# Two interleaved mixers on one core: recurrence scores and masked copies in another order, head output scaled one step later

## The chip, the cores and the metric

The kernel runs on one core of one Trainium2 chip. The metric is the device time of one execution in microseconds (us), lower is better. The engines are called PE (TensorE), DVE (VectorE), ACT (ScalarE), POOL (GpSimd) and SP (SyncE, which here only issues DMAs). Each works through its own instruction list in order and waits on semaphores.

## The reference

Two blocks (`DEPTH = 2`) of a network on 256 context tokens and 256 latent tokens, in fp32, then a gated convolution mixer and a dilated attention mixer. In each block, projections feed three token mixers: a differential attention, a gated linear recurrence (HGRN) in both directions, and a small Fourier mix.

```python
# recurrence, per direction, head and chunk of tokens
rel = where(lower, cum[t] - cum[s], -inf)
scores = einsum('td,sd,tsd->ts', q, k, exp(rel))
o = scores @ v + (q * exp(cum)) @ state
state = exp(cum_end) * state + (k * exp(cum_end - cum)).T @ v
# differential attention, per block of 128 queries and head
s = q @ k.T * DH_A ** -0.5             # two score sets, c = 0, 1
a = softmax(s[0]) - lam * softmax(s[1])
o = rms_norm(a @ v, w) * (1 - lam_init)
```

In block 0 both streams (4 tiles of 128 tokens) get an attention output, 16 pairs of a query tile and a head. In block 1 only the two latent tiles do, 8 pairs.

## The kernel before

Most of the time goes into large products with weights streamed from HBM (each fp32 weight is split into a high and a low part by ACT and DVE, and three products are summed). The change lies in two shorter stages, one per block (`li` = 0 and 1), where the recurrence and the attention run interleaved. Their weights are small; the next weights already wait in their three slots.

**Recurrence.** `hgrn` works through 8 units `i` (direction `d`, token tile `t`, 128 tokens each). In block 1 only units 4 to 7 need outputs (`is_full`), the first four only carry the state. A unit has these parts:

- `gates(i)`: PE transposes k into a PSUM bank (kT, L796), and makes four banks of gate sums (E, L801) and one of suffix sums (L805, L808). ACT takes exponentials (L1375, L1382). DVE copies kT (L1756), multiplies q or k into them (14 instructions at L1772, one at L1773) and makes the decayed keys (L1778, i < 6).
- scores: for 4 pairs `lp` of levels and both row halves `par`, PE writes one PSUM bank with 4 matmuls of 64 rows (L833), 8 banks in all. DVE copies them under masks into `ACC` (L1791, `copy_predicated`, 128x256 each, 16 per unit), one copy per half and level.
- states: PE multiplies `ACC` with the values and adds the state's part (O, L846 and L849), then makes the state's increment (SU, L856, i < 6). DVE copies O (L1808 or L1810) and updates `ST` in four 64x64 blocks (L1820 for i < 2, else L1822).

**Attention.** Step `st` of `attention` handles up to four heads at once: PE makes scores `s` of head u = st (L894), transposes the combined probabilities `aT` of u = st - 1 (L901), multiplies with v (`av`, u = st - 2, L910) and transposes the normed output `oT` of u = st - 3 (L917). DVE finds the row maximum (L1896, two; L1898 scales it by -0.125) and then scales the head output of u = st - 2 into `ON` (L1903). ACT takes the exponentials (L1416), evicts aT (L1223), squares `av` (L1434) and evicts oT (L1440). POOL makes the root of the mean square (L1139, L1141). DVE's `combine` of head u (L1875 to L1880) forms the difference of the softmaxes in place.

**Order.** `weave` merges the lists: after each `yield` of the recurrence it advances the attention so that all its steps (19 in block 0, 11 in block 1) spread over 20 yields; DVE's `combine` of the last head comes at the next yield, or at an early point (`yield True`). For one unit in block 0 this gives

```
PE   gates(i+1) | scores(i) | att a+1 | states(i) | att a+2
DVE  gates(i+1) | combine a | masked copies(i) | att a+1 | states(i) | combine a+1 | att a+2
ACT  gates(i+1) | att a+1 | att a+2
POOL root of head a-1 | root of head a
```

PSUM has 8 banks, given out in turn in PE's order (`open_group`); a bank is written again only when its last reader has counted up the semaphore `taken` of that bank. A score unit takes all 8.

## Time and profile before

| | |
|---|---|
| median of 3 runs | 2212.08 us (2209.62 to 2219.95) |
| the profiled execution's own time | 2207.61 us |
| its span in the trace | 2205.7 us |
| busy share of PE / DVE / ACT / POOL | 89% / 56% / 41% / 3% |
| mean granted TensorE clock | 0.913 of full speed |
| the two interleaved stages | about 272 to 505 us and 1169 to 1298 us |

Busy shares are means over stages with different limits. The granted clock has two levels, 1.0 (2.4 GHz) and 0.5 (1.2 GHz); a mean between them says how the stretch divides.

### The profile page before, as it was taken

Reading aid. Unit: us, or ns where it says so; the run is one execution under the profiler, and the core shown is the slowest. Engines: PE = TensorE matmul, PEld = TensorE weight load, DVE = VectorE, ACT = ScalarE, POOL = GpSimd, SP = SyncE. Lnnn points to the kernel's source line nnn. Section 1 sums busy time; section 2 is a strip of 40 time slices with the busy share of each in tenths; the row PEclk is TensorE's granted clock in tenths of the full one; section 3 lists DMA queues with packets and bytes.
Section 4 is the critical chain, followed back from the end, with each engine's and each line's share of the span. In section 5 each row is a group of like instructions: output and inputs, shape, how many; then the busy total and the mean of one; then the engine's idle time right before and its main releaser. Section 6 shows DMA issues by size and latency. Waiting matters only on the chain.

```text
span 2205.7 us, 27906 instructions
## 1 busy us (share of the span) xinstructions
PE 1956.8 (89%) x11307; PEld 1623.8 (74%) x11307; DVE 1235.3 (56%) x1928; ACT 911.8 (41%) x1213; POOL 74.3 (3%) x135
## 2 busy tenths in 40 slices
PE   4899878868899999998977887989799889999888
PEld 3678656657677777886864566987699869888777
DVE  3553365663666566355545646785566655455684
ACT  4534422222544444325344125564333435566442
POOL 0100000010100000001000010000100000000010
PEclk8899976669999999998987779999899999999998
DMA  7444200001344443323420015554466545555551
GB/s 261 168 147 153 77 1 1 1 1 58 115 153 153 153 153 115 99 81 131 135 94 1 1 57 164 190 173 153 132 186 191 172 158 160 174 165 169 142 66 39
DMA packets 211453, 261.41 MB, mean 119 GB/s; under 512 B 4657, under 2 KB 173283, under 8 KB 211071
## 3 DMA queue, kind: packets, MB, share of 16 engines
q1 hardware_dynamic: 207690, 248.34, 34.7%
q0 software_dynamic: 3232, 11.15, 2.8%
q8 instruction: 90, 1.47, 0.3%
q14 instruction: 36, 0.29, 0.0%
q10 hardware_dynamic: 405, 0.15, 0.0%
HBM read 258.50 MB, written 1.12 MB: 118 GB/s over the span
## 4 chain that ended last, share of the span: by engine, by line
PE 63%; issue 14%; DVE 12%; ACT 5%; DMA 4%; POOL 1%; SPq 0%; DVEq 0%; ACTq 0%; POOLq 0%
PE acc L627 16%; PE acc L629 15%; PE acc L628 15%; DVE scratch L1791 3%; PE acc L801 2%; PE acc L657 2%; PE acc L658 2%; ACT weights_high L1237 1%; DVE weights_low L1625 1%; PE acc L1096 1%; PE acc L846 1%; PE acc L849 1%; DVE mixer_scratch L1772 1%; PE acc L1072 1%; PE acc L1026 1%
## 5 line engine op out<-in xcount | busy, mean ns | idle before, releaser
L1625 DVE TENSOR_TENSOR weights_low<-weights,weights_high 128x2048 fp32r<-128x2048 f32 x232 | 526.6, 2273 | 590.7 <-ACT weights_high L1237 590.6
L1237 ACT ACTIVATE weights_high<-weights 128x2048 fp32r<-128x2048 f32 x232 | 439.9, 1899 | 613.8 <-DMA weights<-in_w_ada_dram 118.2
L627 PE MATMUL acc<-normed_t_high,weights_high 128*128 128x256 f32 (+1 forms) x1824 | 577.6, 317 | 5.3 <-DVE normed_t_low L1659 2.5
L628 PE MATMUL acc<-normed_t_low,weights_high 128*128 128x256 f32 (+1 forms) x1824 | 565.1, 310 | 0.0
L629 PE MATMUL acc<-normed_t_high,weights_low 128*128 128x256 f32 (+1 forms) x1824 | 563.7, 309 | 0.0
L627 PEld LDWEIGHTS acc<-normed_t_high,weights_high 128*128 128x128 f32 x1824 | 346.6, 190 | 37.1 <-DVE normed_t_low L1659 6.9
L628 PEld LDWEIGHTS acc<-normed_t_low,weights_high 128*128 128x128 f32 x1824 | 344.3, 189 | 22.6 <-issue 3.8
L629 PEld LDWEIGHTS acc<-normed_t_high,weights_low 128*128 128x128 f32 x1824 | 344.4, 189 | 20.8
L627 PE MATMUL acc<-weights_high,normed_t_high 128*128 128x512 f32 (+1 forms) x792 | 315.8, 399 | 28.0 <-DVE normed_t_low L1932 27.9
L629 PE MATMUL acc<-weights_high,normed_t_low 128*128 128x512 f32 (+1 forms) x792 | 310.1, 391 | 0.0
L628 PE MATMUL acc<-weights_low,normed_t_high 128*128 128x512 f32 (+1 forms) x792 | 309.9, 391 | 0.0
L627 PEld LDWEIGHTS acc<-weights_high,normed_t_high 128*128 128x128 f32 x792 | 152.0, 192 | 66.7 <-issue 33.2
L628 PEld LDWEIGHTS acc<-weights_low,normed_t_high 128*128 128x128 f32 x792 | 152.2, 192 | 34.7 <-issue 1.4
L629 PEld LDWEIGHTS acc<-weights_high,normed_t_low 128*128 128x128 f32 x792 | 152.0, 192 | 33.6
L1416 ACT ACTIVATE mixer_scratch<-acc,small 128x512 f32<-128x512 f32 (+1 forms) x48 | 29.1, 611 | 229.4 <-DVE small L1898 229.4
L657 PE MATMUL acc<-weights_high,conditioning_split 128*4 128x256 f32 x384 | 99.6, 295 | 16.1 <-DVE weights_low L1625 16.1
L658 PE MATMUL acc<-weights_low,conditioning_split 128*4 128x256 f32 x384 | 99.8, 295 | 0.0
L1473 ACT ACTIVATE scratch<-acc,param_columns 128x512 f32<-128x512 f32 (+1 forms) x88 | 55.6, 664 | 63.3 <-DVE arena L1979 37.9
L1791 DVE COPY_PREDICATED scratch<-level_masks_sb,acc 128x256 f32<-128x256 uint8 x192 | 74.0, 437 | 8.9 <-DVE scratch L1791 6.4
L1932 DVE TENSOR_TENSOR normed_t_low<-arena,normed_t_high 128x512 fp32r<-128x512 f32 (+1 forms) x60 | 50.3, 882 | 47.5 <-ACT normed_t_high L1452 47.4
L648 PE MATMUL acc<-wide_consts,merge_and_gates 128*128 128x128 f32 x144 | 31.5, 390 | 50.9 <-DVE merge_and_gates L1637 50.9
L1452 ACT ACTIVATE normed_t_high<-arena 128x512 fp32r<-128x512 f32 (+1 forms) x60 | 43.6, 777 | 67.1 <-PE acc L629 67.1
(218 smaller groups left out, 2064.0 us busy)
## 6 DMA issues: line engine op xcount, KB each, us to landing
weights<-in_w_ada_dram SPq DMA_DIRECT2D x48, 1024.0 KB, 5.3
weights<-in_w_up_dram SPq DMA_DIRECT2D x44, 1024.0 KB, 5.9
weights<-in_attn_w_in_dram SPq DMA_DIRECT2D x40, 1024.0 KB, 5.1
weights<-in_conv_w_in_dram SPq DMA_DIRECT2D x32, 1024.0 KB, 5.7
weights<-in_w_in_dram SPq DMA_DIRECT2D x24, 1024.0 KB, 6.4
weights<-in_w_down_dram SPq DMA_DIRECT2D x20, 1024.0 KB, 5.0
weights<-in_w_out_dram SPq DMA_DIRECT2D x8, 1024.0 KB, 5.1
weights<-in_conv_w_out_dram SPq DMA_DIRECT2D x8, 1024.0 KB, 5.1
```

Source lines behind the costliest of these rows:

```text
L627: pe.matmul(o, ah, bh, start=start, stop=False)
L628: pe.matmul(o, ah, bl, start=False, stop=False)
L629: return pe.matmul(o, al, bh, start=False, stop=stop)
L657: pe.matmul(o[0:4, 0:256], cond[:, k, :], wh[:, k, :], start=(k == 0), stop=False)
L658: last = pe.matmul(o[0:4, 0:256], cond[:, k, :], wl[:, k, :], start=False, stop=(k == KT - 1))
L801: pe.matmul(o[:, :], GL[:, t, d * 256 + p * P:d * 256 + (p + 1) * P], SM[:, d, 4 * hf:4 * hf + 4, :], start=True, stop=True).then_inc(full, 1)
L1237: act.activation(hi_slot(n)[:, 0:used], slot(n)[:, 0:used], ACT.Copy).then_inc(hi_in.sem, 1)
L1452: act.activation(HH[:, b + k:b + k + 2, lo:lo + X.shape[2]], X[:, r0 + k:r0 + k + 2, :], ACT.Copy).then_inc(part_hi.sem, 1)
L1473: act.activation(FC[:, j, a, 0:w], bank(key, w), ACT.Identity, scale=pcol(("cw", li, 1), a * FT + f), bias=pcol(("cb", li), a * FT + f)).t ...
L1625: dve.tensor_tensor(slot(n, ring_lo)[:, 0:used], slot(n)[:, 0:used], hi_slot(n)[:, 0:used], ALU.subtract).then_inc(lo_in.sem, 1)
L1791: ins = dve.copy_predicated(ACC[:, d, par, :, :], m, bank(key)[:, lv * 256:(lv + 1) * 256].rearrange("p (h n) -> p h n", h=2))
L1932: dve.tensor_tensor(HL[:, b + k:b + k + 2, c], X[:, r0 + k:r0 + k + 2, :], HH[:, b + k:b + k + 2, c], ALU.subtract).then_inc(part_lo.sem, 1)
```

## The change

Six edits, all in the two stages but the last:

1. PE's recurrence sends `scores(i)` ahead of `gates(i+1)`, and DVE's list has the masked copies of unit i first, then `combine`, then `gates(i+1)`.
2. Within a pair of levels the score matmuls go to the two row halves in turn, into two banks.
3. A masked copy covers both banks (128x512) when the two are adjacent; the pair that starts in bank 7 is still copied bank by bank. An extra wait and a semaphore count free the first bank.
4. `ST` holds 128 columns for each pair of heads, so that its update is one instruction (i < 2) or two in place of four.
5. ACT copies the head output out of PSUM into `ON` beside the squares, and DVE scales `ON` in place at the start of step st = u + 3 in place of the end of step u + 2; PE's transpose waits for that.
6. The factor 0.125 goes into the eviction of q, and the maximum is negated by the reduction, so L1898 goes. `combine` loses a wait that others imply.

```diff
-        ST = scr[:, 3584:3840].rearrange("p (d q n) -> p d q n", d=2, q=2)
+        ST = [scr[:, 3584:3840].rearrange("p (q n) -> p q n", q=2), ht_r[:, 3592:3848].rearrange("p (q n) -> p q n", q=2)]
...
+        o_squares = ht_r[:, 3336:3592].rearrange("p (b n) -> p b n", b=2)
...
-                def apply(i):
+                def scores(i):
...
-                            for par in range(2):
-                                o = open_group(("S", li, i, lp, par))
-                                r = slice(64 * par, 64 * par + 64)
-                                for lv in range(2):
-                                    level = 2 * lp + lv
-                                    for p in range(2):
-                                        c = (lv * 2 + p) * P
+                            outs = [open_group(("S", li, i, lp, par)) for par in range(2)]
+                            for lv in range(2):
+                                level = 2 * lp + lv
+                                for p in range(2):
+                                    c = (lv * 2 + p) * P
+                                    for par, o in enumerate(outs):
+                                        r = slice(64 * par, 64 * par + 64)
                                         if level == 0:
                                             zk_, zq_ = KTT[r, b, p, :], QH[r, p, cols_of(t)]
                                         else:
                                             zk_ = zq_ = XE[b][r, p, level - 1, :]
                                         last = pe.matmul(o[:, c:c + P], zk_, zq_, start=True, stop=True)
-                                last.then_inc(full, 1)
-                    yield
+                                        if lv and p:
+                                            last.then_inc(full, 1)
+
+                def states(i):
+                    d, t = un[i]
+                    b = i % 2
...
-                                    last = pe.matmul(o[:, p * 64:(p + 1) * 64], XE[b][r, p, 7, :], ST[r, d, p, :],
+                                    last = pe.matmul(o[:, p * 64:(p + 1) * 64], XE[b][r, p, 7, :], ST[d][r, p, 64 * par:64 * par + 64],
...
                 for i in range(8):
+                    scores(i)
                     if i + 1 < 8:
                         gates(i + 1)
-                    yield from apply(i)
+                    yield
+                    states(i)
...
-                        pe.wait_ge(*taken_after(("av", li, u)))
+                        pe.wait_ge(o_done.sem, o_done.after((li, u)))
...
-                            evict((name, li, 2 * h + m), X[:, 2 * h + m, l0:512], 512 - l0)
+                            key = (name, li, 2 * h + m)
+                            act.wait_ge(full, full_after(key))
+                            act.activation(X[:, 2 * h + m, l0:512], bank(key, 512 - l0), ACT.Copy,
+                                           scale=0.125 if name == "qa" else 1.0).then_inc(taken_of(key), 1)
...
-                            ins = act.activation(E2[:, u % 2, c, 0:n], bank(("s", li, u, c), n), ACT.Exp, scale=0.125,
+                            ins = act.activation(E2[:, u % 2, c, 0:n], bank(("s", li, u, c), n), ACT.Exp,
...
-                        act.activation(ON[:, u % 2, :], bank(("av", li, u), P), ACT.Square,
+                        act.activation(o_squares[:, u % 2, :], bank(("av", li, u), P), ACT.Square,
                                        scale=1.0 / math.sqrt(128.0), accum_out=ossq[:, b]).then_inc(o_sq.sem, 1)
+                        act.activation(ON[:, u % 2, :], bank(("av", li, u), P), ACT.Copy).then_inc(taken_of(("av", li, u)), 1)
...
+                def masked(i):
                     d, t = un[i]
-                    b = i % 2
-                    yield True
                     if is_full(li, i):
                         for lp in range(4):
                             dve.wait_ge(full, full_after(("S", li, i, lp, 1)))
+                            keys = [("S", li, i, lp, par) for par in range(2)]
+                            b0 = group[keys[0]] % BANKS
                             for lv in range(2):
-                                m = MASK[:, d, 2 * lp + lv, :].unsqueeze(1).to_broadcast([P, 2, P])
-                                for par in range(2):
-                                    key = ("S", li, i, lp, par)
-                                    ins = dve.copy_predicated(ACC[:, d, par, :, :], m,
-                                                              bank(key)[:, lv * 256:(lv + 1) * 256].rearrange("p (h n) -> p h n", h=2))
+                                acc = ACC[:, d, :, :, :].rearrange("p a h n -> p (a h) n")
+                                m = MASK[:, d, 2 * lp + lv, :].unsqueeze(1).to_broadcast([P, 4, P])
+                                lvs = slice(lv * 256, (lv + 1) * 256)
+                                if b0 + 1 < BANKS:
+                                    src = ps[:, b0:b0 + 2, lvs].rearrange("p a (h n) -> p a h n", h=2)
+                                    ins = dve.copy_predicated(ACC[:, d, :, :, :], m.rearrange("p (a h) n -> p a h n", a=2), src)
                                     if lv:
-                                        ins.then_inc(taken_of(key), 1)
+                                        ins.then_inc(taken_of(keys[1]), 1)
+                                        dve.wait_ge(*taken_after(keys[1]))
+                                        dve.sem_inc(taken_of(keys[0]), 1)
                                     else:
                                         ins.then_inc(vector_step, line.one())
-                                dve.wait_ge(vector_step, line.n)
+                                        dve.wait_ge(vector_step, line.n)
+                                else:
+                                    for par in range(2):
+                                        ins = dve.copy_predicated(ACC[:, d, par, :, :], m[:, 0:2, :],
+                                                                  bank(keys[par])[:, lvs].rearrange("p (h n) -> p h n", h=2))
+                                        if lv:
+                                            ins.then_inc(taken_of(keys[par]), 1)
+                                        else:
+                                            ins.then_inc(vector_step, line.one())
+                                    dve.wait_ge(vector_step, line.n)
+                                    if lv:
+                                        for key in keys:
+                                            dve.wait_ge(*taken_after(key))
                             for par in range(2):
                                 dve.wait_ge(*taken_after(("S", li, i, lp, par)))
-                    yield
+
+                def states(i):
...
-                        for p in range(2):
-                            for hh in range(2):
-                                r = slice(64 * hh, 64 * hh + 64)
-                                dst = ST[r, d, p, :]
-                                new = bank(key)[r, p * P + hh * 64:p * P + hh * 64 + 64]
-                                if i < 2:
-                                    ins = dve.tensor_copy(dst, new)
-                                else:
-                                    ins = dve.scalar_tensor_tensor(dst, dst, SE[r, b, 256 + p:257 + p], new, ALU.mult, ALU.add)
-                                if p == 1 and hh == 1:
+                        new = bank(key, 256).rearrange("p (q n) -> p q n", q=2)
+                        if i < 2:
+                            dve.tensor_copy(ST[d], new).then_inc(taken_of(key), 1)
+                        else:
+                            for p in range(2):
+                                ins = dve.scalar_tensor_tensor(ST[d][:, p, :], ST[d][:, p, :], SE[:, b, 256 + p:257 + p],
+                                                               new[:, p, :], ALU.mult, ALU.add)
+                                if p:
                                     ins.then_inc(taken_of(key), 1)
...
                 for i in range(8):
+                    masked(i)
+                    yield True
                     if i + 1 < 8:
                         gates(i + 1)
-                    yield from apply(i)
+                    yield
+                    states(i)
                     yield
                 live = range(NT) if li == 0 else range(2, NT)
...
-                    dve.wait_ge(a_max.sem, a_max.after((li, u)))
...
+                    if 0 <= st - 3 < U:
+                        u = st - 3
+                        b = u % 2
+                        dve.wait_ge(o_rs.sem, o_rs.after((li, u)))
+                        dve.wait_ge(*taken_after(("av", li, u)))
+                        dve.tensor_scalar(ON[:, b, :], ON[:, b, :], orstd[:, b:b + 1],
+                                                              1.0 - lam_init, ALU.mult, ALU.mult).then_inc(o_done.sem, 1)
...
-                            dve.tensor_reduce(arec[:, b, c:c + 1], bank(("s", li, u, c), n), AX.X, ALU.max).then_inc(vector_step, line.one())
-                        dve.wait_ge(vector_step, line.n)
-                        dve.tensor_scalar(amax[:, b, :], arec[:, b, :], -0.125, None, ALU.mult).then_inc(a_max.sem, 1)
-                    if 0 <= st - 2 < U:
-                        u = st - 2
-                        b = u % 2
-                        dve.wait_ge(o_rs.sem, o_rs.after((li, u)))
-                        dve.tensor_scalar(ON[:, b, :], bank(("av", li, u), P), orstd[:, b:b + 1],
-                                                              1.0 - lam_init, ALU.mult, ALU.mult).then_inc(taken_of(("av", li, u)), 1)
+                            ins = dve.tensor_reduce(amax[:, b, c:c + 1], bank(("s", li, u, c), n), AX.X, ALU.max, negate=True)
+                            if c:
+                                ins.then_inc(a_max.sem, 1)
+                            else:
```

## Rows read from the trace of the kernel before

**Rows 1.** Busy time by stretch; columns PE, PEld, DVE, ACT, POOL, clock, DMA.
```profile
272.31:318.58 46.27, 35.25 (x216) 25.66 (x215) 32.59 (x113) 10.89 (x25) 0.00 (x0) 0.78 0.00 1
318.58:401.28 82.70, 69.58 (x370) 51.31 (x369) 49.19 (x166) 18.92 (x62) 4.73 (x12) 0.69 0.00 1
401.28:476.08 74.80, 62.77 (x357) 45.55 (x356) 46.85 (x139) 19.25 (x56) 4.73 (x12) 0.73 0.00 1
476.08:504.79 28.71, 12.78 (x57) 10.09 (x55) 13.64 (x36) 9.39 (x28) 9.33 (x16) 0.62 0.00 1
1168.88:1201.07 32.19, 25.55 (x91) 16.90 (x92) 20.50 (x63) 8.79 (x23) 0.79 (x2) 0.66 0.00 1
1201.07:1227.63 26.56, 19.91 (x115) 14.55 (x115) 14.88 (x47) 5.00 (x13) 0.79 (x2) 0.71 0.00 1
1227.63:1298.35 70.72, 55.43 (x345) 43.11 (x344) 43.79 (x131) 17.88 (x52) 7.76 (x16) 0.78 0.00 1
```

**Rows 2.** Waits, 264 to 504 us: total us, times, longest.
```profile
DVE mixer_scratch L1903 <- POOL small L1141: 45.4, 15, 4.4
DVE scratch L1772 <- ACT scratch L1375: 13.3, 4, 4.7
```

**Rows 3.** The same view, 1165 to 1305 us.
```profile
DVE mixer_scratch L1903 <- POOL small L1141: 22.6, 7, 3.3
```

**Rows 4.** Timeline of DVE, 401 to 430 us: start, duration; idle before in brackets.
```profile
407.30 0.29 DVE L1772 TENSOR_TENSOR scratch<-scratch 128x128 f32<-128x128 f32 x1 [2.34 <-ACT scratch L1375]
...
413.70 1.58 DVE L1791 COPY_PREDICATED scratch<-level_masks_sb,acc 128x256 f32<-128x256 uint8 x4 [0.20 <-DVE scratch L1791]
...
423.74 0.35 DVE L1903 TENSOR_SCALAR mixer_scratch<-acc,small 128x128 f32<-128x128 f32 x1 [3.22 <-POOL small L1141]
...
424.77 1.22 DVE L1822 SCALAR_TENSOR_TENSOR scratch<-scratch,mixer_scratch,acc 64x64 f32<-64x64 f32 x4 [0.28 <-PE acc L856]
```

**Rows 5.** Groups by line and shape, whole run: two row maxima, and the copy.
```profile
L1896 DVE TENSOR_REDUCE small<-acc 128x1 f32<-128x512 f32 x32 | 20.6, 685 | 3.3 <-PE acc L894 1.9 <-DVE scratch L1791 1.2
L1896 DVE TENSOR_REDUCE small<-acc 128x1 f32<-128x256 f32 x16 | 6.0, 419 | 1.1 <-DVE scratch L1791 0.8 <-PE acc L894 0.2
L1791 DVE COPY_PREDICATED scratch<-level_masks_sb,acc 128x256 f32<-128x256 uint8 x192 | 74.0, 437 | 8.9 <-DVE scratch L1791 6.4 <-PE acc L917 0.4 <-PE acc L894 0.2
```

**Rows 6.** Timeline of two masked copies, DVE, 412.2 to 412.6 us.
```profile
411.93 0.76 DVE L1791 COPY_PREDICATED scratch<-level_masks_sb,acc 128x256 f32<-128x256 uint8 x2
```

**Rows 7.** Timeline of PE, 401 to 425 us.
```profile
401.85 4.69 PE L801 MATMUL acc<-wide_consts,arena 128*128 128x512 f32 x8
...
407.24 0.27 PE L833 MATMUL acc<-arena,scratch 64*128 64x128 f32 x1
407.24 0.27 PE L833 MATMUL acc<-mixer_scratch 64*128 64x128 f32 x1
...
407.57 3.93 PE L833 MATMUL acc<-mixer_scratch 64*128 64x128 f32 x52
...
418.61 0.66 PE L846 MATMUL acc<-arena,scratch 128*128 128x64 f32 x2 [1.29 <-DVE scratch L1791]
...
423.51 1.22 PE L856 MATMUL acc<-arena,mixer_scratch 128*128 128x128 f32 x4
```

**Rows 8.** Timeline of PE, 424 to 431 us.
```profile
427.71 1.09 PE L901 MATMUL acc<-wide_consts,mixer_scratch 128*128 128x128 f32 x4 [0.97 <-DVE mixer_scratch L1880]
428.59 1.91 PE L910 MATMUL acc<-arena 128*128 128x128 f32 x8
430.30 0.42 PE L917 MATMUL acc<-wide_consts,mixer_scratch 128*128 128x128 f32 x1
```

**Rows 9.** Timeline of PE, 447 to 451 us, one unit later.
```profile
447.69 0.44 PE L846 MATMUL acc<-arena,scratch 128*128 128x64 f32 x2
```

**Rows 10.** Busy time by stretch, columns as in rows 1.
```profile
404.00:414.00 10.00, 8.28 (x73) 6.19 (x72) 7.07 (x26) 2.19 (x4) 0.25 (x1) 1.00 0.00 0
414.40:431.30 16.90, 14.58 (x50) 10.87 (x50) 10.18 (x28) 4.63 (x16) 0.79 (x2) 0.50 0.00 1
```

5 lines of the change are left out of this document (4 added, 1 removed).

## Prediction

> **What bounds the kernel now.** I read the page first, then busy time by stretch: the change acts only in the two interleaved stages, 362 us in seven stretches [rows 1]. No DMA runs there (share 0.00) and the next weights already wait, so what these stages lose or gain passes to the end one for one. DVE is busy 221.5 us of the 362 (sum of the third pair of columns), PE 281.3. Neither is full: they take turns. The waits say for what. DVE waits 45.4 us in the first stage and 22.6 us in the second for POOL's root before it may scale a head output (L1903) [rows 2, 3], and 13.3 us for ACT's exponentials of the gate sums before L1772 on one of its two buffers [rows 2]. The timeline of a unit shows why [rows 4]: after the row maxima, DVE stands 3.22 us until softmax exponentials, squares and root of an older head have passed through ACT and POOL, which themselves had waited for those maxima. This happens twice a unit; before L1772 it stands 2.34 us. It hardly waits for PE (0.28 us before L1822), because PE's output products run under the root wait. So the root wait hides another, and this is what the sum must respect.
>
> **Terms of the instructions.** *Masked copies.* Two 128x256 copies take 0.76 us [rows 6] at 0.437 each [rows 5]; four and the wait behind them take 1.58 + 0.20 = 1.78 us [rows 4]. A 128x512 copy is not in the trace. Upper bound: two copies without overlap, 0.87. Lower bound: one copy plus 256 more elements, which cost a row maximum 685 - 419 = 266 ns [rows 5]: 0.70. I take 0.70, since it is the same work a column. Two of them, 0.04 between, and 0.27 behind (the 0.20 and one more count) make 1.71 us for a pair of levels: 0.07 less, 0.3 us a unit. At 0.87 a pair would take 2.05, 1.1 us a unit more than now, 13 us over 12 units. By the banks that PE's new order gives out, 6 of the 48 pairs start in bank 7 and stay as they are.
>
> The Trainium skill ("VectorE: DVE Perf Modes", section "The DRAIN you can't avoid") says that the next DVE instruction waits until the pipe is empty and that a semaphore between two costs nothing extra. Rows 6 speak against it here: the second copy starts before the first ends. By that rule a merge would save 0.87 - 0.70 = 0.17 us, 14 us over 84 merged copies, where the rows give 0.06 us each, 5 us.
>
> *State update:* 1.22 us for four [rows 4]. Two of 128 partitions by 128 columns cost 0.62 (64 columns more at the maxima's rate, once overlapped): 0.6 us less a unit. *L1898* goes, about 0.2 us for each of 24 heads. *ACT* gets a 128x128 copy per head, about 0.3 us, 7 us in all; ACT is busy 90 us of 362 [rows 1], and the copy lies in front of nothing that DVE awaits within 3 us. The factor in q's eviction, the negated maximum and the dropped wait cost nothing: the same instructions run.
>
> **Moved work.** With the masked copies first, ACT can do the gate exponentials under them, so the wait before L1772 goes. With the scaling a step later, its root is ready: squares end on ACT about 3 us after the maxima, POOL needs under 1 us, and DVE comes back to scale at least 6 us after the maxima. Both root waits go. What is late next:
>
> (a) *O and SU.* PE transposes `oT` just before `states(i)`, and that transpose now waits for DVE's scaling, which stands behind all of `gates(i+1)`. O and SU therefore start only then: 418.61 to 424.73, 6.1 us [rows 7], at the lower clock. With the transpose (0.42, [rows 8]) and a hop, DVE gets its increment 6.6 us after scaling. In between it has one or two maxima pairs' work (0.76 or 1.29 us) and the O copies (0.5): a new wait of 5.4 us for 256 keys, 4.9 for 512. Units 6 and 7 have no SU (1.2 us): 3.7.
>
> (b) *Scores.* PE's `scores(i+1)` come behind `aT`, `av`, `oT` of the step before, which start when DVE's `combine` ends: 1.1 + 1.7 + 0.4 us [rows 8], less for 256 keys. The first pair of banks then takes 8 matmuls, 16 records. Records on the two halves start at the same moment (both 407.24) where a bank ends and the next begins [rows 7], and else come at 3.93 / 52 = 0.076 us; in turn I put them at 0.055, 0.9 us. DVE has 1.1 or 1.65 us of scaling and maxima meanwhile: a wait of 2.1 us for 256 keys, 2.65 for 512. Later pairs come faster than DVE copies them (1.71 us), so only the first quarter of the alternation is on the path: 0.3 us a unit.
>
> The Trainium skill ("TensorEngine Tiling (Array Packing)", section "PSUM Bottleneck") says that tiling speeds TensorE but not the evacuation of PSUM. That would have the alternation give nothing; by the rows it gives 12 x 0.3 = 4 us.
>
> (c) *Gate sums.* E needs banks that masked copies free. With four banks of scores in front, the last E can start 5.1 us after the masked copies do (three pairs) and, at the higher clock, ends under them. No wait.
>
> **The sum, stretch by stretch [rows 1].** New time = DVE busy, less the savings, plus the waits, plus 1.4 us a unit of small gaps (0.8 of it the four 0.20).
>
> - 272.3 to 318.6, units 0 and 1: busy 32.6 - 2.2. Waits: 2.9 for the first exponentials, 1.1 for the first scores, 0.7 for the second gates, 0.3. With gaps 36.9 for 46.3: -9.4. It gains most, because O runs there before any scaling exists and so under DVE's gates.
> - 318.6 to 401.3, units 2 to 4: 49.2 - 3.6 + 3 x 7.5 + 4.2 = 72.3 for 82.7: -10.4.
> - 401.3 to 476.1, units 5 to 7: 46.9 - 2.4 + 4.2 + 7.5 + 6.4 + 8.6 (unit 7 has no gates to run under, so O and its own transposes stand bare) = 71.2 for 74.8: -3.6.
> - 476.1 to 504.8, the drain: two root waits of 3.2 go, 22.2 for 28.7: -6.5.
> - 1168.9 to 1201.1, states only: two updates and the maxima shorter, the extra copy on ACT: -1.3.
> - 1201.1 to 1227.6, unit 4: 14.9 - 1.2 + 1.4 + 0.9 + 0.8 + 0.4: 17.1 for 26.6, -9.5. No attention step stands between gates and states here, so O runs under the gates.
> - 1227.6 to 1298.4: 43.8 - 2.4 + 4.0, waits 3.2, 4.9, 3.7, 3.7 and 1.2, end 3.2: 65.3 for 70.7, -5.4.
>
> Together -46.1 us. The profiled execution took 2207.6 us, so 2161.5 by its measure; it lies 4.5 us under the median of the runs, 2212.1, from which the forecast is 2166.
>
> **Rivals.**
>
> *TensorE at 2.4 GHz for O (faster).* The clock was 0.50 in 414.4 to 431.3 and 1.00 in 404 to 414 [rows 10]; an O pair takes 0.66 us at the one and 0.44 at the other [rows 7, 9], starts 0.62 and 0.36 apart. If the denser order lifts the clock before O, each O takes 2.9 for 4.9 us: 12 x 2.0 off, 2142. Against it: PE still idles some 2 us for the scaling just before O.
>
> *Late gate sums.* The eight records of E took 4.69 us [rows 7], begun at the lower and ended at the higher clock [rows 10]; by the ratio of two I put 6.8 us at the lower alone and 3.4 at the higher. If E runs at 1.2 GHz behind the scores, the last exponential comes 1.8 us after DVE is ready, in some ten units: 2184.
>
> *The waits change only their names.* If (a) and (b) together take what the root and exponential waits took, the saved DVE instructions alone stay, 1.3 us a unit, 16 us: 2196. For it: PE is busy 281 of 362 us, so there is not much slack. Against it: in units 0 and 1, in unit 4 of block 1 and in the drain nothing takes their place.
>
> *Slower: scores and gate sums both at 1.2 GHz.* Place: PE between `oT` and the last E. Scores would take 6.8 us, E 6.8 more in front of DVE's gates: the exponentials end 18 us after `combine` where DVE is ready at 12.9, and O moves along. A period of 27.8 becomes about 30.7, over 11 units +33: 2245. It decides once E ends 3 us later than forecast. Against it: in the unit shown the scores fell into the higher clock after some us of unbroken work [rows 7, 10], and PE now runs from O through the scores almost without a gap.
>
> *The wide copy costs 0.87 us:* +13 against the forecast, 2180.
>
> **Chances.** Forecast 0.48 (own range 2154 to 2178); higher clock 0.11; late gate sums 0.17; only names 0.12; wide copy dear 0.05; slower 0.07. To leave out no more than 0.2, the range runs from 2150 (half the clock gain, which cuts off most of that rival) to 2198, over the names case. One measurement tells about 0.5%, 11 us, from no change. Faster than 2201: all but the slower case and part of the names case, 0.86; within 0.5%: 0.07; slower: 0.07.
>
> **What would show it.** In the new profile the scaling waits for POOL nowhere; L1772 hardly waits for ACT; DVE waits for PE's O and SU near 5 us in units 2 to 6 and about 2 to 3 us before the first masked copy; a wide copy takes 0.70 us; a unit of block 0 takes 24 to 25 us for 27.5; the drain has lost 6 us; clock in these stages stays near 0.7. The prediction is wrong if DVE stands before L1772 or if the O block starts later than the scaling asks.

## The result, and the profile after

The changed kernel takes 2154.5 us (median of 4 runs, 2152.48 to 2163.66), the kernel before in the same comparison 2210.85 us (4 runs). The ratio is 0.9753, 95% interval 0.9732 to 0.9774: 2.5% faster. The forecast was 2166 us with a range of 2150 to 2198, so it was 11.5 us too slow. The profiled execution took 2155.4 us, its span is 2153.6 us, the mean clock 0.925.

Busy time by stretch of the changed kernel, cut at the same places of the program as [rows 1]. The columns are the stretch and its length, then busy us and number of instructions of PE, PEld, DVE, ACT and POOL, the granted clock, the DMA share and GB/s:

```profile
272.49:310.87 38.38, 28.43 (x215) 20.79 (x214) 30.15 (x90) 10.87 (x26) 0.00 (x0) 0.92 0.00 1
310.87:384.82 73.95, 62.68 (x379) 47.18 (x379) 45.21 (x131) 19.95 (x69) 4.75 (x12) 0.72 0.00 1
384.82:454.90 70.08, 57.68 (x353) 41.79 (x351) 44.31 (x111) 20.28 (x63) 4.75 (x12) 0.73 0.00 1
454.90:474.85 19.95, 9.44 (x56) 7.64 (x55) 13.15 (x35) 10.11 (x32) 9.60 (x16) 0.91 0.00 0
1138.07:1164.84 26.77, 21.62 (x105) 13.83 (x105) 17.77 (x49) 8.57 (x25) 1.16 (x2) 0.81 0.00 0
1164.84:1181.32 16.48, 15.86 (x119) 12.03 (x117) 13.71 (x38) 5.39 (x15) 0.79 (x2) 0.90 0.00 1
1181.32:1240.87 59.55, 47.86 (x336) 36.99 (x332) 42.16 (x105) 19.29 (x58) 8.57 (x16) 0.82 0.00 1
```

| stretch | before | forecast | after |
|---|---|---|---|
| units 0, 1 | 46.3 | 36.9 | 38.4 |
| units 2 to 4 | 82.7 | 72.3 | 74.0 |
| units 5 to 7 | 74.8 | 71.2 | 70.1 |
| drain | 28.7 | 22.2 | 20.0 |
| block 1, states only | 32.2 | 30.9 | 26.8 |
| block 1, unit 4 | 26.6 | 17.1 | 16.5 |
| block 1, rest | 70.7 | 65.3 | 59.6 |
| both stages | 362.0 | 315.9 | 305.2 |

The stages gave 56.8 us where 46.1 were forecast. The rest of the program took 1848.4 us in this execution and 1843.7 in the one before; over all profiled executions of this study it lies between 1837 and 1848 us, though of the edits only the factor in q's eviction lies in it. That is why the experiments below are read first by the sum of the two stages, and by the median second. Each sum of stages comes from one profiled execution, and how much it varies from one execution to the next was not measured; where a difference of a few us rests on it alone, this is said.

The waits of the first stage (264 to 480 us), to be held against [rows 2]. Columns: who waited, for whom, us in total, times, longest:

```profile
...
DVE merge_and_gates L1840 <- PE acc L855: 18.0, 8, 4.0
PE acc L925 <- DVE mixer_scratch L1924: 15.1, 7, 2.9
DVE scratch L1805 <- PE acc L835: 12.9, 11, 3.4
DVE merge_and_gates L1838 <- PE acc L855: 8.0, 4, 2.2
DVE scratch L1815 <- PE acc L835: 6.6, 2, 3.5
...
DVE mixer_scratch L1924 <- POOL small L1149: 2.6, 3, 1.0
```

The gate products have two buffers, and [rows 2] shows the wait for the exponentials of one; this is the kernel before on the other, in the same stretch:

```profile
DVE mixer_scratch L1772 <- ACT mixer_scratch L1375: 9.5, 4, 3.3
```

The 45.4 us for POOL's root (now L1924) are 2.6. The 22.8 us for the gate exponentials (13.3 + 9.5, now L1784) are 4.3: 2.9 and 1.4, once each, in front of the gates of units 0 and 1. In their place stand DVE's waits for O (L1838, L1840), 26.0 us, and for the scores (L1805, L1815), 19.5 us. The second row shown is the cause of the first: PE's transpose of the normed output (L925) waits for DVE's scaling (L1924) behind the gates.

One unit of block 0 in the timeline of DVE (start, us, engine, line, operation, out<-in, shapes, count, idle before):

```profile
338.28 1.59 DVE L1815 COPY_PREDICATED scratch<-level_masks_sb,acc 128x256 f32<-128x256 uint8 x4 [3.09 <-PE acc L835]
340.10 1.49 DVE L1805 COPY_PREDICATED scratch<-level_masks_sb,acc 128x512 f32<-128x512 uint8 x2 [0.23 <-DVE scratch L1815]
...
350.39 0.28 DVE L1924 TENSOR_SCALAR mixer_scratch<-mixer_scratch,small 128x128 f32<-128x128 f32 x1
...
353.41 0.29 DVE L1840 TENSOR_TENSOR merge_and_gates<-acc,merge_and_gates 128x128 f32<-128x128 f32 x1 [2.08 <-PE acc L855]
355.88 0.29 DVE L1840 TENSOR_TENSOR merge_and_gates<-acc,merge_and_gates 128x128 f32<-128x128 f32 x1 [2.18 <-PE acc L855]
357.03 0.61 DVE L1849 SCALAR_TENSOR_TENSOR mixer_scratch<-mixer_scratch,acc 128x128 f32<-128x128 f32 x2 [0.86 <-PE acc L862]
```

and the same unit on PE:

```profile
336.13 1.23 PE L835 MATMUL acc<-arena,scratch 64*128 64x128 f32 x8
337.15 4.24 PE L835 MATMUL acc<-mixer_scratch 64*128 64x128 f32 x56
341.60 3.60 PE L803 MATMUL acc<-wide_consts,arena 128*128 128x512 f32 x8
...
350.73 0.48 PE L925 MATMUL acc<-wide_consts,mixer_scratch 128*128 128x128 f32 x1 [2.94 <-DVE mixer_scratch L1924]
351.00 0.53 PE L852 MATMUL acc<-arena,scratch 128*128 128x64 f32 x2
```

DVE scales at 350.39, PE transposes at 350.73 and only then begins O; DVE gets its three pieces after 2.08 + 2.18 + 0.86 = 5.1 us of waiting. After the maxima before, it stands 3.09 us until the first masked copy. The whole gate sums E (L803) took 3.60 us and end at 345.2 (granted clock 1.00 from 341.6 to 345.2), when DVE has just ended its masked copies and has `combine` to do.

The granted clock in five short stretches of the changed kernel: the first and the later scores of that unit, its O and SU, and two O blocks of block 1.

```profile
336.13:338.50 2.37, 2.37 (x23) 2.37 (x24) 0.22 (x1) 1.07 (x7) 0.79 (x2) 0.50 0.00 0
338.50:341.30 2.80, 2.80 (x46) 2.70 (x44) 2.50 (x6) 0.00 (x0) 0.00 (x0) 0.89 0.00 0
351.07:357.07 6.00, 6.00 (x23) 4.83 (x22) 0.89 (x4) 1.98 (x9) 0.79 (x2) 0.50 0.00 0
1194.97:1199.12 4.15, 4.15 (x18) 3.36 (x17) 1.23 (x4) 2.62 (x9) 0.79 (x2) 0.61 0.00 0
1213.51:1216.28 2.77, 2.77 (x21) 2.30 (x22) 1.19 (x3) 1.83 (x6) 0.00 (x0) 1.00 0.00 0
```

The other units differ. Over the first 2.1 us of its scores a unit of block 0 is granted 0.50 in three of the eight (from 311.7, 336.1 and 360.6), 0.72 to 0.77 in three, and 1.00 in two. O runs at 1.00 in units 0 and 1, and at 0.50 to 0.54 in the six units of block 0 behind them.

### The profile page after: what moved, and what is told of

It reads as the page before. It is cut to its first block, busy times and chain, and to the rows that moved or that the text cites. A ratio compares the mean times of both kernels' runs of the same rounds, so it can differ in the third digit from the quotient of the medians.

```text
span 2153.6 us, 27861 instructions
## 1 busy us (share of the span) xinstructions
PE 1925.2 (89%) x11307; PEld 1603.4 (74%) x11307; DVE 1220.8 (57%) x1792; ACT 916.8 (43%) x1237; POOL 75.9 (4%) x135
## 3 DMA queue, kind: packets, MB, share of 16 engines
q8 instruction: 91, 1.49, 0.3%
## 4 chain that ended last, share of the span: by engine, by line
PE 65%; issue 14%; DVE 10%; ACT 5%; DMA 4%; POOL 1%; SPq 0%; DVEq 0%; ACTq 0%; POOLq 0%
PE acc L629 16%; PE acc L630 16%; PE acc L631 16%; PE acc L659 2%; PE acc L835 2%; PE acc L660 2%; ACT weights_high L1245 1%; PE acc L1104 1%; DVE weights_low L1637 1%; DVE scratch L1805 1%; PE acc L803 1%; PE acc L855 1%; DMA weights<-in_w_up_dram 1%; PE acc L852 1%; DVE scratch L1784 1%
## 5 line engine op out<-in xcount | busy, mean ns | idle before, releaser
L629 PEld LDWEIGHTS acc<-normed_t_high,weights_high 128*128 128x128 f32 x1824 | 347.8, 191 | 33.6 <-issue 7.3
L630 PEld LDWEIGHTS acc<-normed_t_low,weights_high 128*128 128x128 f32 x1824 | 346.2, 190 | 23.3 <-issue 4.3
L1965 DVE TENSOR_TENSOR normed_t_low<-arena,normed_t_high 128x512 fp32r<-128x512 f32 (+1 forms) x60 | 50.4, 882 | 45.0 <-ACT normed_t_high L1464 45.0
L1805 DVE COPY_PREDICATED scratch<-level_masks_sb,acc 128x512 f32<-128x512 uint8 x84 | 61.2, 729 | 22.3 <-PE acc L835 15.1
```

Source lines behind the costliest of these rows:

```text
L629: pe.matmul(o, ah, bh, start=start, stop=False)
L630: pe.matmul(o, ah, bl, start=False, stop=False)
L1805: ins = dve.copy_predicated(ACC[:, d, :, :, :], m.rearrange("p (a h) n -> p a h n", a=2), src)
L1965: dve.tensor_tensor(HL[:, b + k:b + k + 2, c], X[:, r0 + k:r0 + k + 2, :], HH[:, b + k:b + k + 2, c], ALU.subtract).then_inc(part_lo.sem, 1)
```

## The experiments

Each kernel is timed against the kernel before in the same comparison, on the same chip. The last three ran on another chip than the kernel with the output transpose moved, so they are compared with it by ratios and stages. The row "before" gives one median of the kernel before; in the other comparisons it was 2210.75 to 2211.24. "Stages" is the length of the two stages in the profiled execution, from DVE's first instruction there (L1861 in the changed kernel) to its first split of rows behind them (L1965), read by the same two instructions in every kernel.

| kernel | median us | ratio, 95% interval | stages us |
|---|---|---|---|
| before | 2210.3 | 1 | 362.0 |
| scaling a step later alone | 2202.9 | 0.9959, 0.9946 to 0.9972 | 355.6 |
| new order alone | 2179.1 | 0.9854, 0.9832 to 0.9877 | 331.2 |
| new order and later scaling | 2176.3 | 0.9844, 0.9822 to 0.9865 | 325.6 |
| **changed kernel** | 2154.5 | 0.9753, 0.9732 to 0.9774 | 305.2 |
| without alternation | 2164.8 | 0.9796, 0.9776 to 0.9815 | 317.9 |
| with narrow copies only | 2151.5 | 0.9736, 0.9716 to 0.9756 | 305.0 |
| four state blocks, maximum negated apart | 2159.4 | 0.9758, 0.9735 to 0.9781 | 311.4 |
| `combine` behind the gates | 2166.7 | 0.9802, 0.9779 to 0.9826 | 321.6 |
| output transpose behind the states | 2129.3 | 0.9627, 0.9607 to 0.9648 | 282.1 |
| the same, without alternation | 2133.4 | 0.9644, 0.9627 to 0.9661 | 292.6 |
| the same, narrow copies only | 2132.2 | 0.9633, 0.9613 to 0.9653 | 281.8 |
| all later head parts behind the states | 2122.2 | 0.9601, 0.9567 to 0.9636 | 277.7 |

**The scaling a step later, alone.** The old order on PE and DVE, the scores half by half, narrow copies, the old state update and L1898 back; only edit 5 is left, and of edit 6 the factor in q's eviction and the dropped wait, which stay in every kernel of this section.

```diff
                 for i in range(8):
-                    scores(i)
                     if i + 1 < 8:
                         gates(i + 1)
+                    scores(i)
                     yield
```

> Only the scaling of the head output moves a step later (with ACT's extra copy); order, copies, maxima and state updates as before. Theory: in the old order each of the two root waits of a unit covers another wait that ends within some tenths of a us of it (O and SU before the state update, the gate exponentials before L1772), so units 2 to 6 gain nothing and only the drain of each stage gains: 6 to 9 us in all, ratio 0.996. Rival (the 68 us of root waits are really idle time): most of them go, 40 to 60 us, ratio 0.973 to 0.982.

Measured: 2202.9 us, stages 355.6, that is 6.4 us of the 68 us of root waits [rows 2, 3], as its theory expected. Where the rest went stands in this kernel's waits of the first stage:

```profile
DVE scratch L1784 <- ACT scratch L1386: 16.6, 4, 4.8
DVE mixer_scratch L1784 <- ACT mixer_scratch L1386: 15.0, 4, 5.7
DVE merge_and_gates L1840 <- PE acc L855: 12.8, 8, 2.2
DVE merge_and_gates L1838 <- PE acc L855: 7.6, 4, 2.2
```

DVE now stands 31.6 us for the gate exponentials of both buffers, against 22.8, and 20.4 us for O, against 1.5; with the state's increment that is 27.1 against 7.6. These the root wait had covered. So the root wait covered two others, as the prediction's first part says; the edit that takes away the largest wait of the profile is worth 0.4% by itself.

**The new order alone.** Edit 1 is left; DVE scales at the end of step u + 2 as before, and the other edits are undone as above.

```diff
-                        pe.wait_ge(o_done.sem, o_done.after((li, u)))
+                        pe.wait_ge(*taken_after(("av", li, u)))
```

> Only the order changes: scores ahead of the gate sums on PE, masked copies ahead of combine and gates on DVE. The head output is scaled as before, straight from PSUM at the end of its step, so DVE waits for POOL's root again, but PE's transpose no longer waits for a scaling behind the gates, and O starts some 3 us earlier. Theory: the root wait of 3.2 us stands where the O wait of 5 us stood, the two orders cost nearly the same in units 2 to 6, the drains do not gain: 38 to 48 us faster, ratio 0.979 to 0.983. Rival (each part brings its own share, scaling a third or more of the whole): 25 to 35 us, ratio 0.985 to 0.989.

Measured: 2179.1 us, stages 331.2, so 30.8 us off. Its waits, the first row of the first stage and the first of the second:

```profile
DVE mixer_scratch L1934 <- POOL small L1149: 45.4, 15, 4.4
DVE mixer_scratch L1934 <- POOL small L1149: 22.6, 7, 3.3
```

Both root waits stand there with the same sums as in [rows 2] and [rows 3], and the time fell by 31 us all the same: this order takes away what stands in front of the gates, and leaves the roots. DVE's waits for gate exponentials were 33.8 us over both stages before (22.8 and 11.0) and are 3.7 here. The theory had expected 38 to 48 us and was too high; the gain is in its rival's range, 25 to 35, but not for its rival's reason, since the later scaling adds only what the next run shows.

**Order and later scaling together.** Edits 1 and 5.

> Order and late scaling together; copies bank by bank, scores half by half, four state updates and the separate scaling of the maximum as before. Theory: about 1.1 us a unit for the narrow instructions and 0.2 for each head, 13 to 18 us, is missing against the whole change: 38 to 44 us faster than before, ratio 0.980 to 0.983, the same as the order alone within a few us. Rival (the instruction edits are hidden under PE's waits): ratio 0.975 as the whole change.

Measured: 2176.3 us, stages 325.6: 5.6 us of stage time on top of the order. The two medians differ by 2.8 us and their intervals overlap, so that the scaling brings anything on top of the order is likely, not shown. It is 34 us faster than the kernel before, just under the 38 to 44 expected. The root waits are down to 2.8 us in the first stage, and DVE stands 23.3 us for scores and 23.3 us for O (15.7 at L1840, 7.6 at L1838) there instead. The order and the scaling together are 36.4 of the 56.8 us; the small edits must hold the other 20.4. Undone one by one in the next three runs, they come to 12.7, -0.2 and 6.2.

**Without alternation.** The changed kernel with PE's four matmuls of one bank sent ahead of those of the next.

```diff
-                            for lv in range(2):
-                                level = 2 * lp + lv
-                                for p in range(2):
-                                    c = (lv * 2 + p) * P
-                                    for par, o in enumerate(outs):
-                                        r = slice(64 * par, 64 * par + 64)
+                            for par, o in enumerate(outs):
+                                r = slice(64 * par, 64 * par + 64)
+                                for lv in range(2):
+                                    level = 2 * lp + lv
+                                    for p in range(2):
+                                        c = (lv * 2 + p) * P
```

> The whole change, but the score matmuls of a pair of banks go out half by half as before. The prediction took the scores at the higher clock and gave the alternation 0.3 us a unit, 4 us. The profile after shows them begun at the lower clock, where half by half the first pair takes about 2.4 us for 1.7 and the later pairs about 1.85 us each, more than a masked copy needs. Theory: 0.7 us for the first pair and 0.1 to 0.2 for each later one, 10 to 16 us slower than the whole change: 2165 to 2171 us, ratio 0.979 to 0.982. Rival (the prediction's own term): 4 us, 2158, ratio 0.977.

Measured: 2164.8 us, stages 317.9: the alternation is worth 12.7 us of stage time, where the prediction had 4. By the medians it is 10.3, at the low end of the 10 to 16 expected. The first two masked rows of a unit without it, and the clock in this kernel's scores (339.98 to 347.95, cut in two):

```profile
343.04 1.58 DVE L1815 COPY_PREDICATED scratch<-level_masks_sb,acc 128x256 f32<-128x256 uint8 x4 [4.07 <-PE acc L835]
345.18 1.49 DVE L1805 COPY_PREDICATED scratch<-level_masks_sb,acc 128x512 f32<-128x512 uint8 x2 [0.56 <-PE acc L835]
```

```profile
339.98:342.50 2.52, 2.52 (x18) 2.52 (x19) 0.00 (x0) 1.00 (x6) 0.79 (x2) 0.50 0.00 0
342.50:347.95 5.45, 5.45 (x52) 5.33 (x49) 3.98 (x8) 0.00 (x0) 0.00 (x0) 0.65 0.00 0
```

The 64 records take 8.0 us (339.91 to 347.89) where the changed kernel takes 5.3 (336.13 to 341.39). DVE waits 4.07 us for the first pair against 3.09, and 0.56 for the second. The scores open at the lower clock in both, and there the half-by-half order is slow enough to be felt in the second pair too. It also leaves the lower clock later: the spacing of the records halves 3.0 us into the scores in the changed kernel, and 6.4 us into them here.

One unit opens at 1.00 in both kernels, so it shows the order at the higher clock. First the changed kernel, then this one:

```profile
384.33 0.71 PE L835 MATMUL acc<-arena,scratch 64*128 64x128 f32 x8
385.57 1.50 DVE L1805 COPY_PREDICATED scratch<-level_masks_sb,acc 128x512 f32<-128x512 uint8 x2 [0.82 <-PE acc L835]
```

```profile
391.11 0.71 PE L835 MATMUL acc<-arena,scratch 64*128 64x128 f32 x4
392.86 1.49 DVE L1805 COPY_PREDICATED scratch<-level_masks_sb,acc 128x512 f32<-128x512 uint8 x2 [1.74 <-PE acc L835]
```

From the first record to the first masked copy it is 1.24 us in turn and 1.75 half by half, 0.51 us more; at the lower clock it is 2.15 and 3.13, 0.98 us more (336.13 to 338.28, 339.91 to 343.04). So the first pair alone costs twice as much at the lower clock, and at the higher one still more than the 0.3 us of the prediction.

**Narrow copies only.** The changed kernel with every pair copied bank by bank.

```diff
-                                if b0 + 1 < BANKS:
+                                if b0 < 0:
```

> The whole change, but every masked copy is made bank by bank (128x256, 16 a unit). A wide pair group takes 1.68 us in the profile after, a narrow one 1.78 to 1.81: 0.4 us a unit, 3 to 6 us slower than the whole change: 2157 to 2161 us, ratio 0.976 to 0.978. Rival (the page's rule, 0.17 us a copy): 14 us, ratio 0.982.

Measured: 2151.5 us, stages 305.0, where 3 to 6 us slower was expected: the wide copy is worth nothing that shows. A pair of levels in this kernel's timeline, and the group of the wide copies in the changed kernel (columns: busy us, mean ns, idle before and its releasers):

```profile
340.45 1.59 DVE L1815 COPY_PREDICATED scratch<-level_masks_sb,acc 128x256 f32<-128x256 uint8 x4 [0.23 <-DVE scratch L1815]
```

```profile
L1805 DVE COPY_PREDICATED scratch<-level_masks_sb,acc 128x512 f32<-128x512 uint8 x84 | 61.2, 729 | 22.3 <-PE acc L835 15.1 <-DVEq L1809 4.1 <-PE acc L803 0.5
```

Four narrow copies and the gap take 1.59 + 0.23 = 1.82 us, two wide ones 1.49 + 0.24 = 1.73. DVE's busy time in the stages is 210.2 us with narrow copies (135.4 + 74.8) and 206.5 with wide ones (132.8 + 73.6), 3.8 us less, and none of it reaches the stages' length.

**Four state blocks, and the maximum negated apart.** Edits 4 and 6 (but for the factor in the eviction and the dropped wait) are undone, by the lines of before.

```diff
-                            ins = dve.tensor_reduce(amax[:, b, c:c + 1], bank(("s", li, u, c), n), AX.X, ALU.max, negate=True)
+                            dve.tensor_reduce(arec[:, b, c:c + 1], bank(("s", li, u, c), n), AX.X, ALU.max).then_inc(vector_step, line.one())
+                        dve.wait_ge(vector_step, line.n)
+                        dve.tensor_scalar(amax[:, b, :], arec[:, b, :], -1.0, None, ALU.mult).then_inc(a_max.sem, 1)
```

> The whole change, but the state is updated in four 64x64 blocks and the row maximum is negated by an instruction of its own. Terms of the prediction: 0.6 us for each of 12 updates and 0.17 to 0.2 us for each of 24 heads, all on DVE's own path: 8 to 12 us slower than the whole change, 2163 to 2167 us, ratio 0.979 to 0.981. Rival (hidden under PE's waits): under 4 us, ratio below 0.977.

Measured: 2159.4 us, stages 311.4: 6.2 us for the two together, between the 8 to 12 expected and the rival's under 4. By the medians it is 4.9 us, with overlapping intervals, so the size is not shown. By the terms of the prediction they save 12 x 0.6 + 24 x 0.2 = 12.0 us of DVE's work. A likely reason, which no run of its own shows, is that the maxima stand in front of the wait for O, and what is saved ahead of a wait is waited.

**`combine` behind the gates.** The changed kernel with DVE's early point moved.

```diff
                     masked(i)
-                    yield True
                     if i + 1 < 8:
                         gates(i + 1)
+                    yield True
                     yield
```

> The whole change, but DVE does combine of the head behind the gates of the next unit instead of between masked copies and gates. Theory: its place is worth much, because PE's transposes, products and then O wait for it, and because in block 1 it fills the wait for the gate exponentials: O starts 1.5 to 2.5 us later in 11 units and block 1 loses 2 to 4 us more, 18 to 30 us slower than the whole change, 2173 to 2185 us. Rival (DVE does the same work in another order, PE has slack): within 5 us of 2154.

Measured: 2166.7 us, stages 321.6, 16.4 us more than the changed kernel and 12.2 by the medians: clearly more than the rival's 5, and less than the 18 to 30 expected. In the states-only part of block 1, from DVE's first instruction to its first masked copy, this kernel takes 1147.80 to 1179.58, 31.8 us, where the changed one takes 27.2 (1137.99 to 1165.14). Three waits of its second stage show why:

```profile
DVE merge_and_gates L1838 <- PE acc L855: 6.1, 2, 4.0
DVE scratch L1784 <- ACT scratch L1386: 4.7, 2, 3.9
DVE mixer_scratch L1790 <- ACT mixer_scratch L1393: 4.1, 2, 2.3
```

With `combine` ahead of the gates, DVE works on the heads while ACT makes the exponentials. The changed kernel waits at L1784 and L1790 for 1.2 us in its second stage.

**The output transpose behind the states.** The prediction's wait (a) taken away without touching DVE: PE sends the transpose of the normed output behind `states(i)`, from a list of its own.

```diff
-                    if 0 <= st - 3 < U:
-                        u = st - 3
-                        pe.wait_ge(o_done.sem, o_done.after((li, u)))
-                        o = open_group(("oT", li, u))
-                        pe.transpose(o[:, 0:P], ON[:, u % 2, :], ident).then_inc(full, 1)
                     yield
+            def heads_out(li):
+                ...
+                        pe.transpose(o[:, 0:P], ON[:, u % 2, :], ident).then_inc(full, 1)
+                    yield
...
                 for i in range(8):
+                    yield True
                     scores(i)
...
-                weave(hgrn(li), attention(li), mixer_steps(li))
+                late = heads_out(li)
+                weave(hgrn(li), attention(li), mixer_steps(li), late)
```

> The whole change, but PE sends the transpose of the head output behind the states of the unit (in the step before the first scores it stays where it was), so O and SU no longer wait for DVE's scaling behind the gates. Theory of the prediction's part (a): O starts about 3 us earlier, DVE's wait before the state update falls from 5.7 to about 2.5 us in some 8 units, 20 to 28 us faster than the whole change: 2127 to 2135 us, ratio 0.962 to 0.966. Rival (the transpose is not what holds O, or ACT's later eviction of it holds the next step): no change against 2154.

Measured: 2129.3 us (2124.49 to 2131.38), stages 282.1: 23.1 us less than the changed kernel, as expected. PE and DVE of one unit:

```profile
341.59 0.33 PE L852 MATMUL acc<-arena,scratch 128*128 128x64 f32 x2
```

```profile
344.55 0.75 DVE L1942 TENSOR_REDUCE small<-acc 128x1 f32<-128x256 f32 x2
345.21 0.48 DVE L1849 TENSOR_TENSOR merge_and_gates<-acc,merge_and_gates 128x128 f32<-128x128 f32 x2
345.61 0.60 DVE L1858 SCALAR_TENSOR_TENSOR mixer_scratch<-mixer_scratch,acc 128x128 f32<-128x128 f32 x2
```

O and SU run from 341.6 to 345.1 under DVE's multiplications, and DVE's copies of O (L1849) and the state update (L1858) follow the maxima without a gap. The clock in this kernel's first scores, later scores, and O with SU:

```profile
330.45:332.50 2.05, 2.05 (x26) 2.05 (x28) 0.26 (x1) 1.54 (x9) 0.77 (x2) 0.69 0.00 0
332.50:334.92 2.42, 2.42 (x44) 2.30 (x42) 2.12 (x6) 0.00 (x0) 0.02 (x1) 1.00 0.00 0
341.59:345.11 3.52, 3.52 (x23) 2.85 (x21) 3.52 (x16) 0.00 (x0) 0.00 (x0) 1.00 0.02 5
```

With PE no longer standing 2.94 us in front of O, O and SU are granted 1.00 and take 3.5 us where they took 6.0 at 0.50; so do they in all of units 2 to 5. The scores do not share in this: in block 0 their first 2.1 us are still granted 0.50 in three units (from 311.1, 349.4 and 390.4), and the unit shown, with 0.69, is one of three between the levels. Both effects came with the one edit; a run that has the wait gone and the low clock kept was not made.

**The same, without alternation.** It asks whether the alternation is dear because the scores open at the lower clock.

> TensorE's transpose of the normed output behind the states, as in the 2129 us kernel, and the scores half by half. Question: is the alternation dear because the scores open at the lower clock? In the changed kernel it was worth 12.7 us of the two stages, where the prediction said 4 and where TensorE's first 2.3 us of a unit's scores were granted 0.50. With the transpose moved the clock in that stretch is 0.69 in the one unit read. Theory (the price of the half-by-half order is set by the low clock of the first bank alone): it shrinks with the low stretch, 5 to 9 us over the 2129 kernel, 2134 to 2138, scores' first masked copy 0.5 to 0.7 us later per unit. Rival (the price is set by the whole of the scores, which must keep ahead of the masked copies, whatever the clock): 12 us or more, 2141 or above.

Measured: 2133.4 us, stages 292.6. By stage time the alternation is worth 10.5 us here, against 12.7 in the changed kernel; by the medians 4.1, with overlapping intervals. The stage time lies between what the two theories expected, and the run can't decide between them, because the low clock that it was to take away is still there. The 0.69 was read in one unit, and in this kernel the scores of that same unit open at the lower clock:

```profile
335.21:337.31 2.10, 2.10 (x15) 2.10 (x15) 0.00 (x0) 1.63 (x9) 0.73 (x2) 0.50 0.04 8
```

They do so in four of the eight units of block 0, against three in the changed kernel. What the clock does to the price is seen unit by unit instead: here too the first pair takes 3.14 us from the first record to the first masked copy where the scores open at 0.50, and 1.75 in the unit that opens at 1.00 (from 375.49); in turn it is 2.15 and 1.24. How much of the 12.7 us is the low clock stays open.

**The same, narrow copies only.**

> TensorE's transpose behind the states and all masked copies one bank wide. In the changed kernel the wide copy gave nothing (2151.5 against 2154.5), and two reasons were left: the instruction itself costs as much as two narrow ones (729 ns against 0.76 us for two), or a saving of 0.2 us a unit was eaten by the wait for TensorE's output products. Here those products run under VectorE's multiplications, so there is no such wait to eat it. First reason: 2127 to 2131 again, stage lengths within 1.5 us of the 282.1 us of the 2129 kernel. Second: stages 3 us or more longer, 2132 or above.

Measured: 2132.2 us, stages 281.8 against 282.1. The wait for O is all but gone, and the wide copy still gives nothing by the stages, so the wait for O did not eat its saving. The first reason of the expectation, that the wide instruction costs as much as two, holds to 0.03 us a copy (729 ns against 0.76), but with the gaps the rows say 0.09 us a pair, and DVE is busy 4.2 us longer with narrow copies (209.6 against 205.3). Most of this is in another wait: for scores DVE waits 22.3 us over both stages with wide copies (18.0 and 4.3) and 18.7 with narrow ones (15.2 and 3.5). With wide copies DVE is ready sooner and PE is not. Between the changed kernel and its narrow form the same two waits, for scores and for O, differ by 2.3 us (55.8 against 53.5).

**All later head parts behind the states.** PE sends only the attention's scores `s` between gates and states; `aT`, `av` and `oT` come behind `states(i)`.

```diff
                 for i in range(8):
+                    yield True
                     scores(i)
...
                             pe.matmul(o[:, 0:nk_], QA[r, h, cols_of(t)], KA[r, h, 0:nk_], start=True, stop=True).then_inc(full, 1)
+                    yield
+
+            def heads_out(li):
+                au = att_units(li)
+                U = len(au)
+                for st in range(U + 3):
                     if 0 <= st - 1 < U:
...
-                weave(hgrn(li), attention(li), mixer_steps(li))
+                late = heads_out(li)
+                weave(hgrn(li), attention(li), mixer_steps(li), late)
```

> TensorE sends only the attention's scores between the gate sums and the states; the transposes of the combined probabilities, their product with the values and the transpose of the normed output all come behind the states. Theory (with the output transpose gone from there, TensorE's path to O waits for nothing of VectorE that is late, so the two other parts need not move; they only take TensorE 1.1 + 1.1 us ahead of O, under VectorE's multiplications): no gain from O; the squares and the root of that head come some 4 us later, and the scaling of the next step waits for POOL instead, and the scores of the next unit start later, behind two steps' transposes: 2130 to 2145. Rival (O's start is still what the states wait for): 2118 to 2126, 0.6 us a unit or more off.

Measured: 2122.2 us, stages 277.7, 4.4 less than with the transpose alone (177.3 + 100.3 against 182.1 + 100.0, so all of it in block 0). The runs spread from 2115.81 to 2134.46 and the interval overlaps that of the kernel it is compared with: the step is likely, not shown. Its waits in block 0:

```profile
DVE scratch L1815 <- PE acc L835: 10.1, 9, 3.3
DVE mixer_scratch L1934 <- POOL small L1159: 8.2, 9, 2.4
```

The time is in the rival's range (2118 to 2126) and not in the theory's (2130 to 2145), which expected no gain from O. Of its mechanism a part is there: the waits for POOL rise from 4.8 to 8.2 us as the theory expected, and PE reaches O and the next scores sooner, so that DVE's waits for scores fall from 18.0 (12.2 and 5.8) to 12.9 (10.1 and 2.8) and the 5.9 for O fall to 1.7.

## Why the prediction came out right

Sign, mechanism and order of size hold: the root waits covered others, and the new order removed these. That the total came within 11.5 us is in part luck, since its parts were off in both directions: units 0 to 4 took 3.1 us longer than forecast, the other stretches 13.8 less. These are its steps.

**The root waits cover others.** Right, and shown from both sides: the later scaling alone brings 6.4 us of 68, the order alone brings 30.8 with both root waits untouched and 30.1 us less of waits for gate exponentials.

**Wait (a), O behind the scaling.** Right: 5.4 us forecast for 256 keys, 5.1 in the unit shown; in the first stage DVE waits 26.0 us for O. It is the largest thing that the change leaves, and moving one transpose brings 23.1 us, by the shorter stand and the higher clock together. The rival of O at 2.4 GHz did not come in block 0 (0.50 to 0.54 in units 2 to 7), but in part in block 1, where of the two O blocks shown above one ran at 1.00 and one at 0.61. That is one part of the 59.6 us there for 65.3.

**Wait (b), before the first scores.** The mechanism is right, the size is not. The prediction took 2.1 and 2.65 us; DVE stands 3.07 to 3.46 us in five of the six units of block 0 with a step before them, and 0.82 in the sixth, whose scores run at 1.00. The term that was too small is the first pair of banks: 0.9 us forecast for 16 records at 0.055, 2.15 measured from the first record to the first copy at a clock of 0.50. The price of 0.055 us a record is right at the higher clock (44 records in 2.42 us at 1.00), but at the lower one 23 records take 2.37 us. In the unit shown PE comes from O at 0.50, stands 0.81 us for `combine`, and is granted 0.50 for the transposes and the product too.

**The alternation.** The term was mis-sized by three: 4 us forecast, 12.7 measured. The first pair of banks comes 0.98 us later without it at the lower clock, and 0.51 at the higher, where the prediction had 0.3. "Only the first quarter of the alternation is on the path" is wrong at the lower clock: there the second pair of banks is late as well (0.56 us). The rule of the Trainium skill that the prediction set beside the term ("TensorEngine Tiling (Array Packing)", section "PSUM Bottleneck") is not contradicted in what it states, since a pair of wide copies takes 1.49 us in either order. That the alternation would then give nothing is wrong here, because DVE waits for the scores' first banks and not the other way round.

**The wide copy.** The instruction is as forecast, 0.729 us for 0.70, and a pair takes 1.73 for 1.71. The forecast gain of 0.3 us a unit, 3.6 us, does not show in either pair of kernels; in the pair with the transpose moved, DVE's longer waits for scores hold most of it. The rule of the Trainium skill ("VectorE: DVE Perf Modes", section "The DRAIN you can't avoid"), by which the merge would bring 14 us, is out: two stage comparisons give -0.2 and -0.3 us. The same section adds that a next instruction that is not held (not made to wait for the earlier ones) starts earlier. The prediction left this out, and it fits [rows 6], where the second copy starts before the first has ended.

**State update and maxima.** Two blocks take 0.61 us as forecast (0.62), L1898 is gone; 6.2 us reach the end by the stages, of 12.0 saved.

**Gate sums (c).** Right: E takes 3.60 us at the higher clock and ends with the masked copies, ahead of `combine`, and DVE waits for gate exponentials only in units 0 and 1 of the first stage (2.9 and 1.4 us; 2.9 and 0.7 forecast). The rivals of late gate sums and of two slow groups did not come, nor that of waits that only change their names.

**The missed term.** The states-only part of block 1 was forecast at 30.9 us and took 26.8. The prediction counted shorter instructions there and overlooked that `combine` now stands ahead of the gates, under ACT's exponentials. With `combine` behind the gates this part is 4.6 us longer. In the sum over both stages this place is worth 16.4 us, those 4.6 and the rest in other units, where the prediction had the order right without naming that edit.

**The drain.** 22.2 us forecast, 20.0 measured. The prediction let two root waits of 3.2 us go. The trace before has a third one there, of 4.36 us; the three (10.8 us) became 0.79, 0.79 and 1.04, so 8.2 us went.

**The sum.** Units 0 and 1 took 38.4 us for 36.9: the prediction's sum there has 1.5 us of small gaps, where its own 1.4 us a unit would make 2.8 and the forecast 38.2. Smaller slips, 221.5 for a DVE sum of 221.4 and 17.1 for 17.2 in unit 4, change nothing. So the 10.7 us by which the stages did better than forecast lie in block 1 (30.9, 17.1 and 65.3 forecast, 26.8, 16.5 and 59.6 measured: 10.5 us) and in the drain (2.2), while units 0 to 4 did 3.1 us worse, half by the gaps and half as (b) was longer, and units 5 to 7 1.1 better.

## What to carry to other kernels

When one wait dominates a profile, look for what runs underneath it before pricing its removal: here the largest wait was worth 6 us alone, and an order that did not touch it was worth 31. When an operation is moved later in one engine's list, look at everything that another engine has queued behind its consumer; the consumer may be moved as well, which here gave another 23 us, more than any edit of the change but the order. A clock read in one unit is not the clock of all: read every unit before building an experiment on it. Price TensorE's work in a moved place by the clock it will find there, and treat savings ahead of a wait as waited.

## What was not expected of the hardware

- O and SU of a unit take 6.0 us at a granted clock of 0.50 after PE stood 2.94 us, and 3.5 us at 1.00 without that stand. In the unit shown the clock is still 1.00 when PE stops (347.8 to 348.8) and 0.50 before it goes on (349.8 to 350.7). Moving one transpose of 0.4 us changed the level of O in units 2 to 6, but on the whole not that of the scores behind it.
- Score matmuls on the two row halves, sent in turn, take 5.3 us for 64 records, and 8.0 us sent half by half, though both open at 0.50; in turn the records start in pairs, 0.21 us apart at 0.50 and 0.11 at 1.00, while in the half-by-half order the records of different halves overlap only where one bank ends and the next begins.
- A masked copy of 128x512 out of PSUM takes 729 ns, a 128x256 one 441 ns, and two of those in a row 0.76 us: a merge has little to win.
